# Linear-attention values of an encoder layer projected with tokens on partitions, in one double slab

## The reference, cut to what matters

```
h = rms_norm(x); z = h @ w_in                     # one projection, columns split up
gq, gk, gv, gg, ... = split(z)                    # q, k: 4 heads x 128; v, gate: 4 heads x 256
la_f, la_b = log_sigmoid(low_rank @ wa2 + ba)/16  # decays, forward and backward
o_f = gla_direction(q, k, v, la_f, False)         # chunked linear attention, both ways
o_b = flip(gla_direction(flip(q), flip(k), flip(v), flip(la_b), True))
#   per chunk:  o = (q e^b)(k e^-b)^T masked @ v + (q e^b) @ S;   S = e^bl * S + k'^T @ v
```

## Time and profile before

| | |
|---|---|
| median of 3 runs | 2585.76 us (2585.68 to 2587.13) |
| the profiled execution, its own time | 2587.82 us |
| its span, first to last instruction | 2586.2 us |
| mean granted TensorE clock | 0.998 of full speed |
| PE busy | 2550.8 us, 99% of the span |
| DVE, ACT, POOL busy | 59%, 41%, 9% |

### The profile page before, as it was taken

One profiled execution on the slowest core, in us unless ns is written; L12 is line 12 of the kernel. 1 busy time (PEld: TensorE's weight loads), 2 busy tenths in 40 slices (PEclk: granted clock), 3 DMA queues, 4 the chain that ended last, 5 costly groups with the idle time before them and its releaser, 6 DMA issues.

```text
span 2586.2 us, 39809 instructions
## 1 busy us (share of the span) xinstructions
PE 2550.8 (99%) x15178; PEld 2310.2 (89%) x15178; DVE 1535.0 (59%) x2276; ACT 1063.3 (41%) x1727; POOL 241.1 (9%) x403
## 2 busy tenths in 40 slices
PE   7999999999999999999999999999999999999998
PEld 5888888888888888888888888999999999999887
DVE  5545554564554644547443353988878867677743
ACT  5554345441544424544343343633333333333721
POOL 3010000100001000010010011021111300000000
PEclk9999999999999999999999999999999999999999
DMA  3122121221212212122162233144434862442021
GB/s 117 33 26 65 54 75 26 34 74 36 75 34 35 74 45 65 34 26 78 47 256 99 100 112 124 56 155 137 148 128 136 305 214 86 164 148 81 25 74 57
DMA packets 201704, 236.40 MB, mean 91 GB/s; under 512 B 14928, under 2 KB 172176, under 8 KB 201520
## 3 DMA queue, kind: packets, MB, share of 16 engines
q0 software_dynamic: 34576, 138.78, 17.0%
q1 hardware_dynamic: 164864, 95.05, 13.0%
q10 hardware_dynamic: 2080, 0.14, 0.1%
HBM read 168.73 MB, written 65.02 MB: 90 GB/s over the span
## 4 chain that ended last, share of the span: by engine, by line
PE 92%; DVE 4%; issue 2%; ACT 1%; DMA 0%; POOL 0%; POOLq 0%; DVEq 0%; ACTq 0%; SPq 0%
PE banks L1099 18%; PE banks L1101 18%; PE banks L1100 18%; PE banks L1465 5%; PE banks L1467 5%; PE banks L1466 5%; PE banks L1394 4%; PE banks L1395 4%; PE banks L1396 4%; PE banks L1214 2%; PE banks L1195 1%; PE banks L1304 1%; PE banks L1287 1%; PE banks L1205 1%; PE banks L1257 1%
## 5 line engine op out<-in xcount | busy, mean ns | idle before, releaser
L1099 PE MATMUL banks<-act_hi,w_hi 128*128 128x512 f32 (+1 forms) x2400 | 894.7, 373 | 3.5 <-DVE w_lo L2080 2.3
L1101 PE MATMUL banks<-act_hi,w_lo 128*128 128x512 f32 (+1 forms) x2400 | 852.3, 355 | 0.0
L1100 PE MATMUL banks<-act_lo,w_hi 128*128 128x512 f32 (+1 forms) x2400 | 850.9, 355 | 0.0
L1101 PEld LDWEIGHTS banks<-act_hi,w_lo 128*128 128x128 f32 x2400 | 453.1, 189 | 65.6
L1099 PEld LDWEIGHTS banks<-act_hi,w_hi 128*128 128x128 f32 x2400 | 454.2, 189 | 61.4 <-DVE w_lo L2080 3.0
L1100 PEld LDWEIGHTS banks<-act_lo,w_hi 128*128 128x128 f32 x2400 | 455.1, 190 | 53.5
L1465 PE MATMUL banks<-op,ring 128*128 128x320 f32 x896 | 277.3, 309 | 1.4 <-issue 0.8
L1467 PE MATMUL banks<-op,ring 128*128 128x320 f32 x896 | 276.9, 309 | 0.0
L1466 PE MATMUL banks<-op,ring 128*128 128x320 f32 x896 | 276.9, 309 | 0.0
L1748 ACT ACTIVATE work<-banks 128x512 f32<-128x512 f32 (+4 forms) x228 | 113.8, 504 | 341.2 <-PE banks L1101 341.2
L2080 DVE TENSOR_TENSOR w_lo<-w_raw,w_hi 128x1024 fp32r<-128x1024 f32 x110 | 130.2, 1183 | 77.3 <-ACT w_hi L1549 74.2
(11 more groups left out here) (358 smaller groups left out, 4242.8 us busy)
## 6 DMA issues: line engine op xcount, KB each, us to landing
w_raw<-in_w_in_dram SPq DMA_DIRECT2D x76, 512.0 KB
operand_scratch<-work POOLq DMA_DIRECT2D x112, 320.0 KB, 2.7
op_f<-operand_scratch POOLq DMA_DIRECT2D x28, 1280.0 KB, 6.5
w_raw<-in_w_mlp_dram SPq DMA_DIRECT2D x48, 512.0 KB, 5.7
work<-gate_scratch POOLq DMA_DIRECT2D x16, 640.0 KB, 5.4
gate_scratch<-work POOLq DMA_DIRECT2D x15, 640.0 KB, 3.3
raw<-in_w_mlp_dram SPq DMA_DIRECT2D x16, 512.0 KB, 5.6
work<-weight_scratch POOLq DMA_DIRECT2D x12, 640.0 KB, 6.1
```

The lines of the kernel that those rows point to most:

```text
L1099: nc.tensor.matmul(out, wh, rh, start=first and k == 0, stop=False, skip_group_check=True)
L1100: nc.tensor.matmul(out, wh, rl, start=False, stop=False, skip_group_check=True)
L1101: mm = nc.tensor.matmul(out, wl, rh, start=False, stop=k == kt - 1, skip_group_check=True)
```

## The change

The two value slabs become one double slab. The activations' tiles are the stationary operand and 256 weight columns move, so that the product arrives with tokens on partitions.

- SP loads slab 11 as rows k 0 to 3 of all 256 columns, slab 12 as rows k 4 to 7; the bytes of a load stay the same.
- PE (`values`) takes 40 steps of six matmuls of 256 columns in the 48 ticks: five banks' worth (b), two token tiles in each, in bank b % 3. Both slots of the weights are in use nearly to the end. The order is b 0 to 2 with the first half, the same with the second half, then b 3 and 4 likewise.
- ACT evacuates at ticks 284, 289, 294, 308 and 312, straight into work rows 5 and 0, where linear attention now reads them (`keyvals(tile)`).
- The transposes on PE and the copies on DVE go, with their semaphores.
- Slab 13 can be split only when the first of the two slots is free: `split_high` goes from tick 289 to 303 (`T_SPLIT`), `split_low` from tick 290 to 304. As the list of a tick is unchanged otherwise, this is behind the scan of tick 292 on DVE, where it stood ahead of it. SP's load of slab 14 waits for that split.

```diff
-        keyvals = work[:, 12:14, :].rearrange(...)
+        GV, HALF_K = 11, KT // 2
+        VALUE_ROWS = tuple(work[:, r, :].rearrange("p (n v) -> p n v", v=DV) for r in (5, 0))
+        def keyvals(tile):
+            return VALUE_ROWS[tile // 5][:, tile % 5, :]
-        T_VT, T_VN = (322, 325, 330, 334, 337), (327, 328, 334, 340, 341)
+        T_V = 24 * GV
+        V_ORDER = ([(b, k) for e in range(2) for b in range(3) for k in range(HALF_K * e, HALF_K * e + HALF_K)]
+                   + [(b, k) for e in range(2) for b in range(3, 5) for k in range(HALF_K * e, HALF_K * e + HALF_K)])
+        V_ENDS = [i for i, (b, k) in enumerate(V_ORDER) if k == KT - 1 or (b, k) == (4, HALF_K - 1)]
+        T_VALUES = {T_V + 20: (0, 1), T_V + 25: (2, 3), T_V + 30: (4, 5), T_V + 44: (6, 7), T_V + 48: (8, 9)}
+        T_SPLIT = T_V + 39
...
+                    if t in (GV, GV + 1):
+                        k0 = HALF_K * (t - GV)
+                        load(n + t, w_in[:, k0:k0 + HALF_K, bass.ds(C_GV + h * DV, DV)])
...
-                if tick in T_VT:                       # PE: four transposes, five times
-                    ...
+            def values(h, tick):
+                n = N_HEAD + GV + h * SLOTS
+                for i in range(5 * tick // 6, 5 * (tick + 1) // 6):
+                    b, k = V_ORDER[i]
+                    if i in (0, 3 * HALF_K):
+                        pe.wait_ge(w_split, n + i // (3 * HALF_K) + 2)
+                    if k == 0:
+                        pe.wait_ge(evac, slab_chunks(n - 1) + b + 2)
+                    slot, w0 = (n + k // HALF_K) % 2, k % HALF_K * DV
+                    for e in range(2):
+                        tile = slice((2 * b + e) * P, (2 * b + e + 1) * P)
+                        out = bank[b % 3][:, e * DV:e * DV + DV]
+                        wh, wl = w_hi[:, slot, w0:w0 + DV], w_lo[:, slot, w0:w0 + DV]
+                        nc.tensor.matmul(out, act_hi[:, k, tile], wh, start=k == 0 and e == 0, stop=False, ...)
+                        nc.tensor.matmul(out, act_hi[:, k, tile], wl, start=False, stop=False, ...)
+                        mm = nc.tensor.matmul(out, act_lo[:, k, tile], wh, start=False, stop=k == KT - 1, ...)
+                    if i in V_ENDS:
+                        mm.then_inc(mm_done, 1)
...
-                    if r == 1:                         # ACT
+                    if tick == T_SPLIT:
+                        split_high(N_HEAD + t + 1 + h * SLOTS, (N_HEAD + t + 1) % 2, behind=2)
+                    elif r == 1 and t != GV + 1:
                         split_high(N_HEAD + t + 1 + h * SLOTS, (N_HEAD + t + 1) % 2)
...
-                if tick in T_VN:                       # DVE: copies to keyvals, five times
-                    ...
-                    if r == 2:                         # DVE
+                    if tick == (T_SPLIT + 1 if t == GV + 1 else 24 * t + 2):
                         split_low(N_HEAD + t + 1 + h * SLOTS, (N_HEAD + t + 1) % 2)
```

More of the change, by code:

```diff
@@ L292, in encoder @@
         lr_done, y_read, prep_a, prep_d = sem("lr_done"), sem("y_read"), sem("prep_a"), sem("prep_d")
-        gvt_done, gvn_ready = sem("gvt_done"), sem("gvn_ready")
         pre_done, kdn_ready, a_ready = sem("pre_done"), sem("kdn_ready"), sem("a_ready")
@@ L442, in encoder @@
         carry = ar[:, 8, :].rearrange("p (c l) -> p c l", l=P)
-        keyvals = work[:, 12:14, :].rearrange("p a t -> p (a t)").rearrange("p (n v) -> p n v", v=DV)
+        GV, HALF_K = 11, KT // 2
+        VALUE_ROWS = tuple(work[:, r, :].rearrange("p (n v) -> p n v", v=DV) for r in (5, 0))
+        def keyvals(tile):
+            return VALUE_ROWS[tile // 5][:, tile % 5, :]
         o_gla = ar[:, 8:10, :]
@@ L684, in _ @@
                 for t, c in enumerate(cols):
-                    load(n + t, w_in[:, :, bass.ds(c, P)])
+                    if t in (GV, GV + 1):
+                        k0 = HALF_K * (t - GV)
+                        load(n + t, w_in[:, k0:k0 + HALF_K, bass.ds(C_GV + h * DV, DV)])
+                    else:
+                        load(n + t, w_in[:, :, bass.ds(c, P)])
             for j in range(REST):
@@ L1233, in gla_steps @@
                     mm.then_inc(lr_done, 1)
-                if tick in T_VT:
[L1235 to L1246, removed]
                 def prelude(j):
@@ L1280, in gla_steps @@
                     if j == 0:
-                        pe.wait_ge(gvn_ready, 5 * h + 6)
+                        pe.wait_ge(evac, slab_chunks(N_HEAD + GV + 2) + h * (3 * SLOTS) + 1)
+                        pe.wait_ge(prt_read, 30 * h + 31)
+                        pe.wait_ge(o_read, 30 * h + 31)
                         pe.wait_ge(y_read, 2 * h + 3)
@@ L1286, in gla_steps @@
                         if j not in ENDS[d]:
-                            nc.tensor.matmul(bank[4 + d][:, 0:DV], kdn[:, j % 2, d, :], keyvals[:, tile, :],
+                            nc.tensor.matmul(bank[4 + d][:, 0:DV], kdn[:, j % 2, d, :], keyvals(tile),
                                              start=True, stop=True).then_inc(u_done, 1)
@@ L1295, in gla_steps @@
                     for v in range(2):
-                        mm = nc.tensor.matmul(bank[6][:, v * P:v * P + P], keyvals[:, j, v * P:v * P + P],
+                        mm = nc.tensor.matmul(bank[6][:, v * P:v * P + P], keyvals(j)[:, v * P:v * P + P],
                                               amat[:, j % 2, :], start=v == 0, stop=v == 1 and j in BEGINS[0],
@@ L1309, in gla_steps @@
                     prelude(j + 1)
+            def values(h, tick):
[11 more added lines that the diff above has]
+                        wh, wl = w_hi[:, slot, w0:w0 + DV], w_lo[:, slot, w0:w0 + DV]
+                        nc.tensor.matmul(out, act_hi[:, k, tile], wh, start=k == 0 and e == 0, stop=False, skip_group_check=True)
+                        nc.tensor.matmul(out, act_hi[:, k, tile], wl, start=False, stop=False, skip_group_check=True)
+                        mm = nc.tensor.matmul(out, act_lo[:, k, tile], wh, start=False, stop=k == KT - 1, skip_group_check=True)
+                    if i in V_ENDS:
+                        mm.then_inc(mm_done, 1)
             for h in range(H):
@@ L1313, in _ @@
                     t, c, k = tick // 24, tick % 24 // 8, tick % 8
[L1314 to L1320, removed]
+                    if t in (GV, GV + 1):
+                        values(h, tick - T_V)
+                    else:
+                        if k == 0:
+                            if c == 0:
+                                pe.wait_ge(w_split, N_HEAD + t + 1 + h * SLOTS + 1)
+                            behind = (2, 3, 3)[c] if t == GV + 2 else c + 1
+                            pe.wait_ge(evac, slab_chunks(N_HEAD + t - 1) + behind + h * (3 * SLOTS) + 1)
+                        mm = steps((N_HEAD + t) % 2, c, k, k + 1, KT, act_hi, act_lo)
+                        if k == 7:
+                            mm.then_inc(mm_done, 1)
                     for g in range(3):
@@ L1544, in _, with split_high @@
             own = Chain()
-            def split_high(n, slot, width=1024):
+            def split_high(n, slot, width=1024, behind=1):
                 act.wait_ge(w_loaded, 16 * n + 32)
-                act.wait_ge(mm_done, slab_chunks(n - 1) + 1)
+                act.wait_ge(mm_done, slab_chunks(n - 1) + behind)
                 A(w_hi[:, slot, 0:width], w_raw[:, 0:width], ACT.Copy).then_inc(w_high, 1)
@@ L1718, in _ @@
                     t, r = divmod(tick, 24)
-                    if tick % 8 == 0 and tick:
+                    if tick in T_VALUES:
+                        n = N_HEAD + GV + h * SLOTS
+                        b = T_VALUES[tick][0] // 2
+                        chunk_done(n, b + (b > 2))
+                        if b == 0:
+                            act.wait_ge(scores_done, 30 * h + 21)
+                        if b == 2:
+                            act.wait_ge(scores_done, 30 * h + 31)
+                        tiles = T_VALUES[tick]
+                        for part in ((tiles[:1], tiles[1:]) if b == 2 else (tiles,)):
+                            v0 = DV * (part[0] - tiles[0])
+                            dst = VALUE_ROWS[part[0] // 5][:, part[0] % 5:part[0] % 5 + len(part), :]
+                            A(dst, bank[b % 3][:, v0:v0 + DV * len(part)].rearrange("p (n v) -> p n v", v=DV), ACT.Copy).then_inc(evac, 1)
+                    elif tick % 8 == 0 and tick and not T_V < tick <= T_V + 48:
                         tt, c = divmod(tick // 8 - 1, 3)
@@ L1722, in _ @@
                             if tt == 0:
-                                act.wait_ge(gvt_done, 5 * h + 1)
+                                act.wait_ge(o_done, OUTPUTS * h + 1)
                             elif tt < 3:
@@ L1732, in _ @@
                             elif tt == 17:
-                                act.wait_ge(gvt_done, 5 * h + 6)
+                                act.wait_ge(u_done, STATES * h + STATES + 1)
```

(1 more changed line is left out.)

## The result

The changed kernel takes 2602.56 us in the median of six runs (2600.07 to 2604.88), the kernel before, run beside it, 2586.59 (2585.68 to 2587.13): a ratio of 1.0058, 95% interval 1.0047 to 1.0068, or 16.0 us slower. The prediction was +12.1 us and a time of 2597.9, within 2590 to 2604; the measured time lies in the upper part of that range.

The account below looks back on a forecast made before the run. The prediction took PE, busy 99% of the span, as the bound, with DVE full around slabs 12 and 13. Moved split +15.1, transposes -9.0 and clock +6.0 made +12.1 us on the 2585.76 median: 2597.9, range 2590 to 2604.

Parts of the forecast that it names:

- PE's own work: PE at the value slabs: narrower matmuls add 1.14 us a head, dropped transposes save 9.0 us in all.
- The sum of -4.5: PE's work if nothing waited: 4 x 1.14 - 9.0 = -4.5 us.
- where there is room to spare: DVE's five copies of values are saved behind the scans, where saving them doesn't help the split; no gain counted.
- The moved split: DVE's split of slab 13 falls behind the 6.00 us scan; slab 13 starts later in each head, +15.1 us together.
- The 0.58 us by which the combination would be earlier: DVE's attention combination ahead of the scan starts 0.58 us earlier, as PE reaches tick 267's product sooner.
- The clock: PE behind the four gaps at slab 13: granted clock falls, counted as 3.5 falls of 1.7 us, +6.0 us.
- only one gap of that length is there: Said for rival 1: clock falls are rare in the kernel before, with a single 1.74 us gap at head 3's start.
- Behind the split: Slab 14's load and ACT's work move later too, but stay hidden by 1.4 us before PE's `prelude(0)`.
- That the clock stays up: Rival 1: gaps at slab 13 as reckoned, clock falls once at most; +6.1 to 7.8, about 2592 us; chance 0.13.
- that the split isn't late: Rival 2: combination comes over 3 us earlier, only PE's sum remains; -4.5, 2581.3 us; chance 0.06.
- the third rival: PE waits again at `prelude(0)` or slab 14's chunks, 1 to 2 us a head; +16 to +26, about 2606; chance 0.13.

Follow-up runs that it names:

- the late split's run: Kernel before with only DVE's split of slab 13 moved from tick 290 to 304, behind the first scan: 2611.17 us, ratio 1.0097.
- the fillers: Changed kernel with ten 512-column matmuls, whose result nobody reads, on PE ahead of its wait for slab 13's split: 2595.11 us, ratio 1.0030.
- four fillers: Changed kernel with four, not ten, unread matmuls on PE ahead of its wait for slab 13's split: 2597.84 us, ratio 1.0048.

## Why the prediction was right, step by step

- **PE's own work.** Right within the intervals: +4.6 for narrower matmuls (+4.1 measured alone, 3.9 by the double slab's own timeline), -9.0 for the transposes, though alone in the kernel before they give only 6.0, as DVE's list stands in the way there. The sum of -4.5 agrees with what remains when the split is moved ahead of the scan (-3.4, interval -5.7 to -1.0). Wrong was that the copies are saved "where there is room to spare": before, the products behind them ended at 279.58 (276.70 + 2.88, two of them), and PE came at 279.64:

```profile
276.70 2.88 DVE L2298 TENSOR_TENSOR work<-work,ebt 128x1280 f32<-128x1280 f32 x2
```

- **The moved split.** Right in mechanism and place: it follows 6.00 us behind the scan's start and PE 0.05 behind its end. It was isolated from both sides: alone it costs 24.7 us, and without it the change is a gain.
- **The 0.58 us by which the combination would be earlier.** This term was mis-sized, and by the prediction's own sign of being wrong (a combination that moves by more than 0.58) it failed. Its first half held: the reciprocal in the softmax weights comes 0.73 us earlier against the first matmul of slab 11 in all four heads. But from that reciprocal's start on DVE to the combination it took 12.13, 13.69, 13.08 and 11.97 us in the four heads, against 12.33, 11.64, 12.08 and 11.98 before: 2.8 us more, all of it in the store and the broadcast loads. So the combination moved by -0.92, +1.31, +0.27 and -0.75 us against the first matmul of slab 11, next to nothing on average, and the waits came to 12.7 and not 10.5. POOL's and DVE's timelines of head 1 in the changed kernel, where the store took longest, and POOL's before:

```profile
545.00 0.82 POOL L911 DMA_DIRECT2D weight_scratch<-cw  x1 [25.80 <-DVE cw L2291]
549.13 1.65 POOL L916 DMA_DIRECT2D work<-weight_scratch  x3 [3.31 <-DMA weight_scratch<-cw]
...
557.64 1.33 DVE L2321 TENSOR_TENSOR work<-work 128x1024 f32<-128x1024 f32 x1 [6.16 <-DMA work<-weight_scratch]
```
```profile
542.75 0.82 POOL L897 DMA_DIRECT2D weight_scratch<-cw  x1 [26.52 <-DVE cw L2249]
545.49 1.64 POOL L902 DMA_DIRECT2D work<-weight_scratch  x3 [1.93 <-DMA weight_scratch<-cw]
```

The sum took these DMAs as constant. They scatter, but not alike in both orders. Over the profiles of all eight kernels, the four with the double slab have 12.80, 12.85, 12.96, 13.02, 13.08 and 13.69 us among their sixteen heads, while none of the sixteen heads with single value slabs is above 12.33. The means are 12.4 and 12.0, which makes 1.8 us over four heads. So a slow DMA does come more often with the double slab; what makes it so was not tried and stays open.

- **The clock.** Right: it fell behind all four gaps. 3.5 falls of 1.7 were taken, 6.0, and the four slabs show 7.1. Most of the excess is head 1, whose low stretch lasted longer (2.37 lost). That isn't set by the gap alone: in the late split's run the longest gap, 4.41 us, lost 1.73 and that of 4.26 lost 2.29. That the clock is a cost of its own, beside the wait, is shown by the fillers. The term was in part luck: its price and its chance came from one row, and the prediction's "only one gap of that length is there" is wrong. The same profile has a second gap of 1.74 us, without a fall; the clock of the stretch behind it is 1.00:

```profile
2440.10 0.50 PE L1099 MATMUL banks<-p_hi,w_hi 128*128 128x512 f32 x1 [1.74 <-ACT work L2026]
```
```profile
2440.10:2446.00 5.90, 5.90 (x29) 4.99 (x30) 3.71 (x3) 3.74 (x6) 0.00 (x0) 1.00 0.30 89
```

For a gap of that length the profile thus had one fall in two; the four gaps turned out longer.

- **Behind the split.** Right: ACT waited for slab 14's load, but `T_KEND` ended 1.4 us ahead of PE's `prelude(0)`, as reckoned, in head 0; no second wait in any head. Timelines of DVE, ACT and PE of the changed kernel, head 0, beside the earlier trace rows:

```profile
262.44 1.06 ACT L1576 ACTIVATE w_hi<-w_raw 128x1024 fp32r<-128x1024 f32 x1 [6.16 <-DMA w_raw<-in_w_in_dram]
...
278.15 2.89 DVE L2335 TENSOR_TENSOR work<-work,ebt 128x1280 f32<-128x1280 f32 x2
...
282.46 0.60 PE L1258 MATMUL banks<-work 128*128 128x128 f32 x4
```

- **The rivals.** That the clock stays up is ruled out by the four stretches, that the split isn't late by the four waits, and a second wait by the absence of any at L1258. The forecast's +12.1 fell 3.9 short of the measured difference: 2.2 in the waits and 1.1 in the clock, and the rest is within the runs' spread. The measured +16.0 is also the lower end of the third rival's numbers, so the time alone couldn't tell the two apart; the waits do.

## What to carry to other kernels

Where each engine's list is written by hand, an entry that is moved lands behind everything listed in between: its price is the length of that work on its engine, and not its own length. Here one number, the scan's tick, turns +16 us into -3 us, so read what stands between the old place and the new one before giving up a change. A gap on TensorE can cost twice, once as the wait and again as a slow clock behind it. Where such a wait can't be avoided, matmuls whose result nobody reads can cover it: here ten of them in gaps of 2.5 to 4.1 us gave back about 7 of the 16 us, though moving the split gave back all of them. And an engine that is 59% busy over the span was full in the stretch that mattered. Last, a price read from one row should be looked for a second time in the same profile.

## What the runs showed of the hardware beyond what was expected

The granted clock drops to half at gaps of TensorE, but not at every gap. In the eight profiles, behind the first 30 us, it fell at all ten gaps of 2.43 to 4.41 us (four in the changed kernel, four with the late split, one with four fillers, one at a head's start in the kernel without transposes), but not at the one of 2.39. Of the thirteen gaps of 1.6 to 1.9 us it fell at two, that of 1.74 in the earlier trace rows and one of 1.85 in the run with ten fillers. The rows below are that second one, and one of 1.74 us at another head's start, in the run with narrower matmuls, where it didn't fall. Each has the stretch behind it:

```profile
2050.69 0.41 PE L1498 MATMUL banks<-op,ring 128*128 128x320 f32 x1 [1.85 <-issue]
```
```profile
2051.00:2054.00 3.00, 3.00 (x13) 3.00 (x12) 3.00 (x5) 0.00 (x0) 0.55 (x1) 0.50 1.03 388
```
```profile
368.30 0.50 PE L1099 MATMUL banks<-act_hi,w_hi 128*128 128x512 f32 x1 [1.74 <-DVE w_lo L2091]
```
```profile
368.30:374.00 5.70, 5.70 (x25) 4.71 (x26) 0.00 (x0) 0.82 (x1) 0.00 (x0) 1.00 0.37 95
```

In the late split's first head the first matmul behind the gap still ran at full speed (0.50 us, as in the runs with fillers) and the clock was low a little later, at 260 to 262 us, when PE was busy again: so a gap's end doesn't protect the work behind it.

The fixed part of a matmul with a weight load of its own was 12 ns here (2 x 0.1196 against 0.2273 us), and it showed in the total time (+4.1 us for 384 matmuls more), though the columns were the same.
